# Attention: probabilities transposed as they are, outputs multiplied by spread inverse row sums

## The reference

```
s_loc = einsum('bchd,bacwhd->bhcaw', q_r, k_win) + bias
s_ctx = einsum('bchd,bnhd->bhcn', q_r, k_ctx)
p = softmax(concatenate([s_loc, s_ctx], axis=-1), axis=-1)
return einsum('bhcaw,bacwhd->bchd', p_loc, v_win) + einsum('bhcn,bnhd->bchd', p_ctx, v_ctx)
```

## Time and profile before

| what | us |
|---|---|
| median of 3 runs | 1652.58 |
| lowest and highest run | 1649.93, 1652.86 |
| profiled execution, span from first to last instruction | 1651.3 |
| PE busy in the span | 1596.5 (97%) |
| DVE busy | 992.0 (60%) |
| ACT busy | 650.7 (39%) |

### The profile page before, as it was taken

One profiled execution on the slowest core, in us unless ns is written; L12 is line 12 of the kernel. 1 busy time (PEld: TensorE's weight loads), 2 busy tenths in 40 slices (PEclk: granted clock), 3 DMA queues, 4 the chain that ended last, 5 costly groups with the idle time before them and its releaser, 6 DMA issues.

```text
span 1651.3 us, 26022 instructions
## 1 busy us (share of the span) xinstructions
PE 1596.5 (97%) x10120; PEld 1375.8 (83%) x10120; DVE 992.0 (60%) x1583; ACT 650.7 (39%) x1191; POOL 71.5 (4%) x125
## 2 busy tenths in 40 slices
PE   5999999999899999999999999999999899999999
PEld 4888877678799899899989977888887688888887
DVE  5697788544795388358637676877654433343334
ACT  4344454452742144124313343556683322222222
POOL 0431011000000000000000000101100000000000
PEclk9999999999999999999999999999999999999999
DMA  9623400531214411532352131111132233232332
GB/s 359 72 96 103 141 27 26 209 124 59 69 52 158 174 64 59 211 128 77 115 193 76 45 112 52 39 52 39 60 119 90 76 103 113 90 128 98 105 111 106
DMA packets 49605, 170.50 MB, mean 103 GB/s; under 512 B 5601, under 2 KB 5857, under 8 KB 49377
## 3 DMA queue, kind: packets, MB, share of 16 engines
q1 hardware_dynamic: 37104, 127.00, 22.9%
q10 hardware_dynamic: 11632, 41.03, 6.8%
q0 software_dynamic: 768, 1.08, 0.9%
HBM read 164.87 MB, written 4.19 MB: 102 GB/s over the span
## 4 chain that ended last, share of the span: by engine, by line
PE 87%; ACT 5%; DVE 4%; DMA 2%; issue 2%; SPq 0%; ACTq 0%; DVEq 0%
PE PS L652 38%; PE PS L2304 17%; PE PS L2637 8%; PE PS L2428 8%; PE PS L2280 2%; PE PS L2471 2%; PE PS L2258 2%; DMA scr<-in_ada 1%; DVE c_early L1790 1%; PE PS L2489 1%; PE PS L2723 1%; PE PS L2368 1%; PE PS L2724 1%; ACT w_hi L617 1%; PE PS L2587 1%
## 5 line engine op out<-in xcount | busy, mean ns | idle before, releaser
L623 DVE TENSOR_TENSOR w_lo<-raw,w_hi 128x1024 fp32r<-128x1024 f32 (+2 forms) x172 | 191.0, 1111 | 115.4 <-ACT w_hi L617 112.6
L617 ACT ACTIVATE w_hi<-raw 128x1024 fp32r<-128x1024 f32 (+2 forms) x172 | 165.5, 963 | 231.0 <-PE PS L652 193.9
L1486 DVE SCALAR_TENSOR_TENSOR X<-PS,mod,X 128x512 f32<-128x512 f32 (+2 forms) x120 | 75.7, 659 | 227.9 <-PE PS L652 220.7
L652 PE MATMUL PS<-c_hi,w_hi 128*128 128x512 f32 (+1 forms) x672 | 204.8, 359 | 3.3 <-DVE w_lo L623 2.2
L652 PE MATMUL PS<-c_hi,w_lo 128*128 128x512 f32 (+1 forms) x672 | 203.7, 357 | 0.0
L652 PE MATMUL PS<-c_lo,w_hi 128*128 128x512 f32 (+1 forms) x672 | 202.5, 355 | 0.0
L652 PE MATMUL PS<-h_hi,w_hi 128*128 128x512 f32 x368 | 139.4, 386 | 2.7 <-DVE w_lo L623 2.7
L652 PE MATMUL PS<-h_lo,w_hi 128*128 128x512 f32 x368 | 139.0, 385 | 0.0
L652 PE MATMUL PS<-h_hi,w_lo 128*128 128x512 f32 x368 | 139.0, 385 | 0.0
L652 PEld LDWEIGHTS PS<-c_hi,w_hi 128*128 128x128 f32 x672 | 111.2, 189 | 25.2 <-DVE w_lo L623 3.0
L1790 DVE SCALAR_TENSOR_TENSOR c_early<-X,small,c_early 128x798 f32<-128x798 f32 x120 | 126.0, 1050 | 2.9
(11 more groups left out here) (375 smaller groups left out, 3068.7 us busy)
## 6 DMA issues: line engine op xcount, KB each, us to landing
raw<-in_w SPq DMA_DIRECT2D x152, 512.0 KB, 3.3
adaw<-in_ada ACTq DMA_DIRECT2D x40, 512.0 KB, 4.6
scr<-in_ada ACTq DMA_DIRECT2D x24, 512.0 KB, 6.8
adaw<-in_w SPq DMA_DIRECT2D x20, 512.0 KB, 4.1
raw<-in_w SPq DMA_DIRECT2D x24, 384.0 KB, 3.3
h_early<-in_ada SPq DMA_DIRECT2D x12, 512.0 KB, 5.8
scr<-in_ada SPq DMA_DIRECT2D x4, 1024.0 KB, 15.2
c_early<-in_ada SPq DMA_DIRECT2D x4, 1024.0 KB, 19.4
```

What stands on the lines that cost most here:

```text
L617: nc.scalar.activation(w_hi[:, j, 0:tiles], raw[:, j].rearrange("p (k n) -> p k n", k=KT)[:, 0:tiles], ACT.Copy).then_inc(s_hi, 1)
L623: nc.vector.tensor_tensor(w_lo[:, j, 0:tiles], raw[:, j].rearrange("p (k n) -> p k n", k=KT)[:, 0:tiles], w_hi[:, j, 0:tiles].bitcast(f32) ...
L652: last = nc.tensor.matmul(G[j][:, a:b], w[:, j, k], m[:, k, a:b], start=(n == 1), stop=(n == 3 * k_tiles))
L1486: i = V.scalar_tensor_tensor(out=xs, in0=G[j][:, a:b], scalar=gv, in1=xs, op0=ALU.mult, op1=ALU.add)
```

## The change

The transposition no longer divides: `transpose_probs` uses `nc.tensor.transpose` with the plain identity, and `dg` and its semaphore `s_Pn` are gone. In `attend(U)`, ahead of the values, PE multiplies each head's inverse row sums, broadcast over 64 columns, with the identity: the inverse of query c stands then in column c of all 64 feature rows of that head (`RT`, bank 7, columns 128 to 255). ACT copies `RT` to `rt` in SBUF (`inverse_out`), DVE multiplies `OT` by it into `on` (`attn_scaled`), and `attn_hi` and `attn_lo` read `on` instead of `OT`. `OT` is free when `on` is there.

```diff
-        dg, at = carve(c_dn, at, 2, 2, 128)
+        on, at = carve(c_dn, at, 2, 128)
+        rt, at = carve(c_dn, at, 2, 128)
...
+        RT = PS[:, 7, 128:256]
...
@@ attn_views @@
-                return dst, OT[U].rearrange("p (c r) -> p c r", c=16)
-            return c[:, hp, LAT + 128 * (t - 4):LAT + 128 * (t - 3)], OT[U]
+                return dst, on[:, U % 2].rearrange("p (c r) -> p c r", c=16)
+            return c[:, hp, LAT + 128 * (t - 4):LAT + 128 * (t - 3)], on[:, U % 2]
@@ ACT @@
+            def inverse_out(U):
+
+                act.wait_ge(s_RT, U + 1)
+                if U >= 2:
+                    act.wait_ge(s_on, U - 1)
+                nc.scalar.activation(rt[:, U % 2], RT, ACT.Copy).then_inc(s_rt, 1)
+
             def attn_hi(U):
 
-                act.wait_ge(s_O, U + 1)
+                act.wait_ge(s_on, U + 1)
...
                     exponentials(U + 1)
                 if U > 15:
                     probs_out(U)
+                inverse_out(U)
                 if U in LATE:
@@ DVE @@
                 dve.wait_ge(s_E, 2 * U + 2)
+                if U >= 2:
+                    dve.wait_ge(s_O, U - 1)
                 V.reciprocal(tmp(3, U), tmp(2, U)).then_inc(s_rr, 1)
-                dve.wait_ge(s_rr, U + 1)
+
+            def attn_scaled(U):
+
+                dve.wait_ge(s_O, U + 1)
                 if U >= 2:
-                    dve.wait_ge(s_Tr, U - 1)
-                for h in (1, 0):
-                    V.tensor_scalar(dg[:, U % 2, h], ident, tmp(3, U, h), None, ALU.mult).then_inc(s_Pn, 1)
+                    dve.wait_ge(s_ahi, U - 1)
+                    dve.wait_ge(s_alo, U - 1)
+                dve.wait_ge(s_rt, U + 1)
+                V.tensor_tensor(on[:, U % 2], OT[U], rt[:, U % 2], ALU.mult).then_inc(s_on, 1)
...
+                attn_scaled(U)
                 attn_lo(U)
@@ PE, transpose_probs @@
                     if U and h:
                         pe.wait_ge(s_PT, U)
+                        pe.wait_ge(s_rt, U)
                         pe.wait_ge(s_mod, 3 + min(U, ADA_R + 1))
                     elif U and U <= TAIL:
-                        pe.wait_ge(s_alo, U)
-                    pe.wait_ge(s_Pn, 2 * U + 2 - h)
+                        pe.wait_ge(s_on, U)
+                    pe.wait_ge(s_E, 2 * U + 2 - h)
                     for n, (b, c, _) in enumerate(key_blocks(U % 6)):
-                        last = MM(PS[:, 6 + h, 128 * n:128 * n + 128], Pb[:, U % 2, h, c:c + 128], dg[:, U % 2, h],
-                                  start=True, stop=True)
+                        last = nc.tensor.transpose(PS[:, 6 + h, 128 * n:128 * n + 128], Pb[:, U % 2, h, c:c + 128], ident)
@@ PE, attend @@
                 if U > TAIL:
-                    pe.wait_ge(s_alo, U - 1)
+                    pe.wait_ge(s_on, U - 1)
                 if U == TAIL:
                     pe.wait_ge(s_v, 8)
+                pe.wait_ge(s_rr, U + 1)
+                for h in range(2):
+                    last = MM(RT[64 * h:64 * h + 64], tmp(3, U, h).to_broadcast([128, 64]), ident, start=True, stop=True)
+                last.then_inc(s_RT, 1)
@@ PE, before ada_two_turned @@
+                    pe.wait_ge(s_rt, U + 1)
```

More of the change, by code:

```diff
@@ L402, in program @@
         s_sq, s_ss, s_ln, s_rs = sem("qk_square"), sem("qk_sum"), sem("qk_log"), sem("qk_rstd")
-        s_S, s_neg, s_E, s_Pn = sem("scores_ready"), sem("neg_max_ready"), sem("exp_ready"), sem("probs_ready")
+        s_S, s_neg, s_E = sem("scores_ready"), sem("neg_max_ready"), sem("exp_ready")
         s_mx = sem("max_ready")
@@ L411, in program @@
         s_rel = sem('relu_done')
-        s_PTa, s_rr = sem("probsT_full_ready"), sem("rsum_inverse")
+        s_rr = sem("rsum_inverse")
+        s_on, s_RT, s_rt = sem("attn_scaled"), sem("inverse_spread"), sem("inverse_copied")
         s_spill, s_back = sem("x_spilled"), sem("x_back")
```

## The result

| kernel | median us (lowest to highest, runs) | ratio [95% interval] | profiled span |
|---|---|---|---|
| before | 1652.72 (1649.93 to 1653.26, 4) | 1 | 1651.3 |
| after | 1685.47 (1680.26 to 1688.02, 4) | 1.0192 [1.0177, 1.0208] | 1682.3 |

The change makes the kernel 1.9% slower. The forecast was 1675, between 1656 and 1690: the sign and most of the size are as forecast, and the time lies 10.5 us above it. The profiled execution of after took 1684.14 us as a run, 1.8 more than its span.

A forecast was written before the change was run, and what follows sets the result against it. By averages PE bounds attention, but waits in the strictly ordered ACT and DVE queues would outweigh its saved work: span 1651.3 + 19.5 (walk) + 3 (clock) = 1673.8, as the runs' median 1675 us, range 1656 to 1690.

The forecast's parts named there:

- What bounds: Attention stretch: PE the bound by averages, but DVE's fixed order gives a second path, without slack in units 8, 9, 10, 14.
- PE's records: Attention: single-record transpositions save 22.1 us, two spreads a unit add 6.1, so PE's work falls by 16.0 us.
- DVE's `on` and round trip: Each attention unit: `on` takes 0.25 us, and DVE stands still 0.45 us between `on` and `c_lo`, waiting for `c_hi`.
- Units that wait for rstd: Units 2, 4, 8 and 14: rstd queues on ACT behind the spread's copy, costing 1.6 + 1.8 + 1.6 + 2.0 us.
- The formula: Sum of steps in a unit waiting for rstd; unit 2 gives 12.9 us, or 13.3 with a late qk_sum, before 11.7.
- the walk: Unit-by-unit sum of delays at the end of PE's transpositions, T(0) to T(23); attend(23) ends 19.5 us later.
- The split: Units 3, 9 and 12: the weight split waits behind the spread's copy, costing 1.9 + 2.4 + 1.2 us.
- Unit 15 and the tail: Unit 15 loses 3.5 us to v_out and `w_hi`; from unit 16 the attend interval grows from 7.5 to 8.3 us.
- The clock: Attention: PE's idles bring the lower clock level; two falls that count, 3 us, between ends 0 and 15.
- Rival C: Attention: the clock falls on the path at all ten idles, 1675 + 12 = 1687; chance 14%.
- rival A: PE is the bound throughout and the gates are slack: 1652.6 - 16 = 1637; chance of faster 7%.
- The sign for the output projection's start: Behind attention: the first out-projection product, at 347.2 us before, starts at 365 to 370 if the forecast is right.

The follow-up runs named there:

- e8: The changed kernel with products by the identity, two records a block, in place of its transpositions; 1693.10 us, ratio 1.0235 to before.
- e4: The kernel before with plain transpositions and without the scaled identities, outputs left undivided; 1639.62 us, ratio 0.9925 to before.
- e10: The changed kernel with ACT's copy of `RT` moved behind rstd and squares, still ahead of the weight splits; 1662.83 us, ratio 1.0054 to before.
- e1: The changed kernel with ACT's copy of `RT` moved down to directly ahead of `attn_hi(U)`; 1661.89 us, ratio 1.0057 to before.

## Why the prediction was right, and where its size was off

- **What bounds.** Right: PE alone doesn't set the stretch, DVE's order does in part of it. e8 and e4 measure how much: 22.1 us of PE's work are worth 7.6 in after, and 12.7 in before, where the scalings on DVE went as well.
- **PE's records.** Right: 160 transpositions, 8 in 1.02 us; the two spreads 4 records, 0.39 us in the chain with the passage. But the forecast that PE's busy time falls by 16 us, to 194.3, failed: it is 212.3. The 18 us between are nearly all the lower clock level, at which the same work is busy for twice as long. That level held 39.9 of the 250 us, and PE was busy for 34.1 of them, which makes 17 us more, an estimate.
- **DVE's `on` and round trip.** Right: `on` 0.28 or 0.21 in the chain (0.25 taken), the wait for `c_hi` 0.50 (0.45). A slip in what goes: the row at 154.64 in the earlier trace rows has 0.60 us for the two scalings, not 0.44.
- **Units that wait for rstd.** The formula gave unit 2 as 13.3 us from T to T; it was 13.5, with `qk_scale` at T+6.8 as walked. T(9) came 5.8 us later than before, where the walk had +6.8, T(14) 14.1 against +12.1, and up to there the two stay within 2.2 us. ACT's new copy stood idle for 2.5 us in units 2, 8 and 14, as forecast, and for 0.65 in unit 13. DVE's added wait for rstd was 24.1 - 6.5 = 17.6 us.
- **The split.** Wrong in its share: 5.5 us for units 3, 9 and 12. By e10 against e1 the splits cost 3.6 at unit 9 and 3.0 at unit 15. What I had put on unit 3's split went with the copy's place ahead of rstd: e10 moves the copy behind rstd and takes 20.5 us off the loop, what hangs on it and its share of the low clock included, where the walk had 7.0 for rstd. The share of the clock in this is at most 8.5, an estimate: half of the 17.1 us by which the lower level is shorter in e10. The sum held because the walk went from T to T along the late steps, whatever name each delay was given; that it came out near does not prove the parts, and the expectation of e10, made from these parts, missed by 12 us.
- **Unit 15 and the tail.** Too small: from T(14) to T(16) the walk added 5.5 us, 3.5 of them for unit 15; measured are 7.6 (+14.1 to +21.7). From T(16) to T(22) it added 1.4, and measured are 4.4 (to +26.1). PE in unit 15 of after:

```profile
310.04 1.11 PE L2490 MATMUL PS<-const,scr 128*128 128x128 f32 x4 [3.11 <-DVE c_early L1858]
311.47 2.04 PE L2548 MATMUL PS<-c_early,const 128*128 128x512 f32 x2 [0.32 <-ACT X L1037]
...
316.22 1.02 PE L2548 MATMUL PS<-c_early,const 128*128 128x512 f32 x2
```

The column sums, 5.16 us by the earlier trace rows, take 7.4 here (311.47 to 318.9), since the first of them run at half speed: 2.04 us at 311.47 and 1.02 at 316.22 for the same pair. `w_hi` of row 21, which waits behind them for the spread, starts at 319.56.

- **The clock: the term that was mis-sized.** I took 3 us between ends 0 and 15. The loop overran the walk's 19.5 by 9.4 us and the part behind attention by 2.1, in sum 11.5, of which 2.2 stand in unit 15's column sums and 2.1 behind an output projection that begins at 0.50 granted. At these two places the rows show the lower level; that all 11.5 us are the clock is argued from the sum alone, and the walk's own errors lie in it too. The chain of waits gives a ceiling: of the 44.4 us at the lower level up to 381, 34.3 are pieces of PE in the chain, so at most half of these, 17 us, is the clock's, an estimate. The row I leaned on, one idle of 2 us with no fall, was one case, and the waits of after are longer. Rival C, 1687, took its cause from all ten idles; the measured 1685.5 lies between it and the forecast and nearer to C, with seven stretches at the lower level between 126 and 381. C's "busy at about 0.85, as in 966 to 978" misreads a row: PE was busy there for 9.23 of 12 us, 0.77, and 0.86 is the granted clock.
- **Against rival A.** Its condition was slack in units 2, 8, 13 and 14; e10 gives that slack back and ends at +0.5%, and only e4, without the division, comes near A's 1637 (1639.6).

In sum: 1651.3 + 19.5 + 11.5 = 1682.3, the span. The last term is what is left over once the walk is taken off, and not measured by itself. The sign for the output projection's start, 365 to 370, was missed with it: it starts at 376.1.

## What to carry to other kernels

Before adding a step to an engine that runs its instructions in order, ask first when its input will be there, not how long it takes: a copy of 0.28 us that waited for the next product of PE cost 23 us by what stood behind it, and the same copy one unit earlier or behind the reciprocal roots cost a fraction. Price less work on the busiest engine by an experiment that removes it and adds nothing (here 12.7 of 22 us, with DVE's scalings gone too); that is the most which the moved work may cost. And where a change makes the matmul engine idle, add the lower clock to the sum, for what follows the idle too.

## What the runs showed of the hardware

- After PE had been busy for 2.0 of the 5 us to 233 in after, the granted clock was 0.63 in the next 3 us and 0.50 in the 4 behind, though PE was busy for all of those 4. Eight blocks transposed in 1.02 us at the upper level took 1.94 at 234.66:

```profile
234.66 1.94 PE PS L2490 x8
236.60 5.04 PE PS L2446 x18
241.64 0.39 PE PS L2505 x4
```

- A fall also followed shorter idles. PE idled for 2.4 us up to 162.99 and for 1.1 up to 165.13 in after, and the clock granted from 165.5 to 168.9 was 0.50. The earlier trace rows has an idle of 2.0 us with no fall.
- A transposition of 128x128 float32 leaves one record and 0.13 us each when back to back, half of the product by a full identity (0.248).
- The busy time of an engine is no measure of its work when the clock moves: PE had 16 us less work in the stretch and 2.0 us more busy time.
